# The opening of a fused two-block kernel in halves, with four of sixteen modulation tiles as two passes of rounded parts

## What is computed

```python
mod = silu(c) @ w_ada + b_ada            # c and c_ctx; shift = columns 0..1023, scale = columns 1024..2047
h   = rmsnorm(x, norm_mix) * (1 + scale) + shift        # for x with c, for ctx with c_ctx; 256 tokens each, D = 1024
p   = h @ w_in                                          # 39 column tiles of 128
```

## Time and profile before

| | |
|---|---|
| time, median of 3 (lowest, highest) | 1807.76 us (1807.01, 1810.53) |
| the profiled execution | 1811.46 us, span 1809.5 us |
| PE busy | 1758.9 us, 97% |
| DVE busy | 1306.0 us, 72% |
| ACT busy | 1050.5 us, 58% |
| mean granted clock of TensorE | 0.990 |

### The profile page before, as it was taken

One profiled execution on the slowest core, in us unless ns is written; L12 is line 12 of the kernel. 1 busy time (PEld: TensorE's weight loads), 2 busy tenths in 40 slices (PEclk: granted clock), 3 DMA queues, 4 the chain that ended last, 5 costly groups with the idle time before them and its releaser, 6 DMA issues.

```text
span 1809.5 us, 34945 instructions
## 1 busy us (share of the span) xinstructions
PE 1758.9 (97%) x11968; PEld 1588.0 (88%) x11968; DVE 1306.0 (72%) x2592; ACT 1050.5 (58%) x2110; POOL 180.1 (10%) x148
## 2 busy tenths in 40 slices
PE   7999999999899999999999999999999999999998
PEld 1878789999899988888899999999889899999997
DVE  3787457667898979766766666666686757878887
ACT  2545543343456679766655555555657666666666
POOL 0000003410673520000000000000010000010000
PEclk9899999999999999999999999999999999999999
DMA  8533223225445531255555555555444534455553
GB/s 296 182 105 106 82 83 105 82 98 174 150 164 176 179 110 36 94 195 190 196 185 186 187 188 186 188 189 186 162 174 141 191 126 140 166 182 186 185 185 128
DMA packets 77273, 283.34 MB, mean 157 GB/s; under 512 B 8576, under 2 KB 8576, under 8 KB 76928
## 3 DMA queue, kind: packets, MB, share of 16 engines
q1 hardware_dynamic: 77184, 282.16, 45.9%
HBM read 281.08 MB, written 1.05 MB: 156 GB/s over the span
## 4 chain that ended last, share of the span: by engine, by line
PE 82%; DVE 11%; ACT 3%; issue 1%; DMA 1%; POOL 1%; PEld 0%; PEldq 0%; ACTq 0%; SPq 0%; POOLq 0%; DVEq 0%
PE banks L867 19%; PE banks L855 16%; PE banks L946 9%; PE banks L455 8%; PE banks L1102 7%; PE banks L1126 3%; PE banks L646 2%; PE banks L627 2%; DVE split L2314 2%; PE banks L797 2%; DVE arena L2310 2%; PE banks L423 1%; PE banks L635 1%; PE banks L960 1%; DMA arena<-wstream 1%
## 5 line engine op out<-in xcount | busy, mean ns | idle before, releaser
L1444 ACT ACTIVATE split<-arena 128x512 fp32r<-128x512 f32 x492 | 309.0, 629 | 135.0 <-PE banks L855 76.8
L855 PEld LDWEIGHTS banks<-split 128*128 128x128 f32 x2880 | 355.4, 192 | 10.4 <-DVE split L2240 3.1
L867 PE MATMUL banks<-split 128*128 128x512 f32 x1536 | 361.9, 390 | 1.0 <-issue 1.0
L855 PE MATMUL banks<-split 128*128 128x256 f32 x2880 | 358.7, 283 | 3.1 <-DVE split L2240 2.3
L2332 DVE TENSOR_TENSOR split<-arena,split 128x512 fp32r<-128x512 f32 x396 | 270.7, 690 | 105.5 <-ACT split L1444 99.7
L867 PEld LDWEIGHTS banks<-split 128*128 128x128 f32 x1536 | 283.8, 188 | 57.3 <-issue 1.4
L1422 ACT ACTIVATE split<-arena 128x512 fp32r<-128x512 f32 x312 | 194.5, 628 | 117.1 <-PE banks L1102 52.9
L946 PE MATMUL banks<-split 128*128 128x256 f32 x1728 | 217.7, 287 | 4.3 <-DVE split L2410 3.9
L946 PEld LDWEIGHTS banks<-split 128*128 128x128 f32 x1728 | 212.3, 194 | 7.8 <-issue 6.0
L2387 DVE TENSOR_TENSOR split<-arena,split 128x512 fp32r<-128x512 f32 x180 | 123.2, 695 | 66.5 <-ACT split L1422 64.9
L455 PEld LDWEIGHTS banks<-split 128*128 128x128 f32 (+1 forms) x936 | 132.9, 193 | 28.1 <-issue 14.1
(11 more groups left out here) (413 smaller groups left out, 2447.9 us busy)
## 6 DMA issues: line engine op xcount, KB each, us to landing
arena<-wstream SPq DMA_DIRECT2D x525, 512.0 KB, 3.3
arena<-x_t SPq DMA_DIRECT2D x1, 2048.0 KB, 12.8
arena<-matsa SPq DMA_DIRECT2D x1, 1234.0 KB, 6.2
out_t<-arena SPq DMA_DIRECT2D x4, 256.0 KB, 2.0
arena<-mats SPq DMA_DIRECT2D x1, 576.0 KB, 7.9
arena<-crow SPq DMA_DIRECT2D x1, 512.0 KB, 7.0
arena<-rows SPq DMA_DIRECT2D x1, 512.0 KB, 4.0
arena<-mats SPq DMA_DIRECT2D x1, 449.0 KB, 4.3
```

Of the source, the lines that this page charges most:

```text
L855: mm = pe.matmul(ps[:, 4 + b, 0:S], w_parts[:, c, (2 * m + half) % 4, P * k:P * k + P], h_parts[:, e, 4 * half + k, :], start=(half == 0 a ...
L867: mm = pe.matmul(ps[:, 2 * tt + half, :], g_parts[:, e, j % 2, P * tt:P * tt + P], w_parts[:, c, (2 * m + half) % 4, :], start=(first and ...
L1444: act.activation(w_parts[:, 0, (2 * m + half) % 4, :], ring[:, peer_slot(m), 512 * half:512 * half + 512], ACT.Copy).then_inc(sem["w_hi"], 1)
```

## The change

The opening is put in another order, by halves of k:

- **Load order.** mats is no longer loaded ahead of tile 0, but after the modulation's tile 5. The host lays the four groups of w_ada in the order shift 0..511, scale 0..511, shift 512..1023, scale 512..1023, so that the first two groups give all that k 0 to 3 need.
- **Four columns.** silu(c) is stored with two columns of zeros beside it (csT, four columns), and as high and low part side by side (c_parts, four columns). Every modulation matmul now has four stationary columns and four output rows. For tiles 7, 9, 10 and 12 (MOD_SPLIT) the weights are split too: ScalarE writes the high part of the whole tile (mod_hi, 128 x 1024), VectorE the low part (mod_lo), and TensorE makes four fp32r matmuls (high and low of the weights, for each k) instead of two f32 ones. They use the same buffers w_parts as the projection.
- **Columns.** The rows of modrow are turned into columns by two accumulating f32 matmuls with parts of the identity for each 128 columns, which also add the two halves (mod_columns), instead of by one transpose; once after tile 5, 8 and 12, and the last inside in_tile(0) at k = 2.
- **Halves.** VectorE forms the gains twice, of k 0 to 3 and k 4 to 7 (gains). TensorE works column tiles 0 and 1 as k 0 to 3 of both, then k 4 to 7 of both.
- **Work moved to ScalarE.** Modulation of x for k 0 to 3, 6 and 7 and of ctx for k 4 to 7 (modulated, one ACT instruction each). ScalarE's squares now stand behind mod_out(0). VectorE's inversion and normalisation of ctx stand behind column tile 1's low parts.
- The last load of rows counts on another semaphore.

```diff
+MOD_SPLIT = (7, 9, 10, 12)
+MOD_HALVES = 2 * len(MOD_SPLIT)
+HALVES = MOD_HALVES + 2 * 39
...
+        c_parts = split[:, 4 * KT * S:4 * KT * S + 4 * KT].rearrange("p (k e) -> p k e", k=KT)
...
-            sp.dma_start(mats, mats_in).then_inc(sem["params_in"], 16)
...
-            load_freed_by_matmuls(RING, N_WIN + RING)
+            for n in range(RING, RING + 2):
+                sp.wait_ge(sem["tiles_done"], n - RING + 1)
+                sp.dma_start(tile_at(n), wstream[n]).then_inc(loaded[n % RING], 16)
+            sp.dma_start(mats, mats_in).then_inc(sem["mats_in"], 16)
+            load_freed_by_matmuls(RING + 2, N_WIN + RING)
...
-            pe.wait_ge(sem["silu_c"], 1)
-            for i in range(2):
-                for half in range(2):
-                    pe.wait_ge(sem["mod_bank_free"], 2 * i + half + 1)
-                    for q in range(4):
-                        pe.wait_ge(loaded[q], 32 * i + 16 * half + 16)
-                        for k in range(2):
-                            mm = pe.matmul(ps[0:2, half, :], csT[:, 2 * q + k, :], ring[:, q, 512 * k:512 * k + 512],
-                                           start=(q == 0 and k == 0), stop=(q == 3 and k == 1))
-                        mm.then_inc(sem["tiles_done"], 1)
-                    if i and half == 0:
-                        sum_squares(0, 512)
-                for half in range(2):
-                    pe.wait_ge(sem["mod_bank_free"], 2 * i + half + 3)
-                    for t in range(8 * i + 4 * half, 8 * i + 4 * half + 4):
-                        mm = pe.transpose(ps[:, 2, 2 * t:2 * t + 2], modrow[0:2, P * t:P * t + P], ident[0:2, 0:2])
-            mm.then_inc(sem["mod_cols"], 1)
-
-            def in_tile(t, among={}):
+            def mod_tile(n):
+
+                out = ps[0:4, n // 4 % 2, :]
+                if n in MOD_SPLIT:
+                    m = MOD_SPLIT.index(n)
+                    pe.wait_ge(sem["in_lo"], 2 * m + 2)
+                    for k in range(2):
+                        for c in range(2):
+                            mm = pe.matmul(out, c_parts[:, 2 * (n % 4) + k, :], w_parts[:, c, 2 * (m % 2) + k, :],
+                                           start=(n % 4 + k + c == 0), stop=(n % 4 == 3 and k + c == 2))
+                else:
+                    pe.wait_ge(loaded[n % RING], 16 * (n // RING + 1))
+                    for k in range(2):
+                        mm = pe.matmul(out, csT[:, 2 * (n % 4) + k, :], ring[:, n % RING, 512 * k:512 * k + 512],
+                                       start=(n % 4 + k == 0), stop=(n % 4 == 3 and k == 1))
+                mm.then_inc(sem["tiles_done"], 1)
+
+            def mod_columns(g):
+
+                pe.wait_ge(sem["mod_bank_free"], 2 + g + 1)
+                for j in range(4):
+                    out = ps[:, 2 if g < 2 else 6, 8 * (g % 2) + 2 * j:8 * (g % 2) + 2 * j + 2]
+                    row = modrow[0:4, 512 * g + P * j:512 * g + P * j + P]
+                    pe.matmul(out, row, ident[0:4, 0:2], start=True, stop=False)
+                    mm = pe.matmul(out, row, ident[0:4, 2:4], start=False, stop=True)
+                if g % 2:
+                    mm.then_inc(sem["mod_cols"], 1)
+
+            pe.wait_ge(sem["silu_c"], 2)
+            for n in range(16):
+                if n % 4 == 0:
+                    pe.wait_ge(sem["mod_bank_free"], n // 4 + 1)
+                mod_tile(n)
+                if n == 5:
+                    pe.wait_ge(sem["mats_in"], 16)
+                    mod_columns(0)
+                elif n == 6:
+                    sum_squares(0, 512)
+                elif n in (8, 12):
+                    mod_columns(n // 4 - 1)
...
-            for t in range(19):
+            in_tile(0, {2: (mod_columns, 3)}, range(4))
+            in_tile(1, {}, range(4))
+            in_tile(0, {}, range(4, KT))
+            in_tile(1, {}, range(4, KT))
+            for t in range(2, 19):
...
-            act.wait_ge(sem["params_in"], 32)
-            act.activation(csT, col("c2", KT, 2), ACT.Silu).then_inc(sem["silu_c"], 1)
-            act.wait_ge(sem["x_in"], 16)
-            for k in range(KT):
-                act.activation(sq[:, k, :].rearrange("p (c t) -> p c t", c=2), xc[:, :, k, :], ACT.Square).then_inc(sem["squares"], 1)
-
+            act.wait_ge(sem["params_in"], 16)
+            link(act.activation(csT[:, :, 0:2], col("c2", KT, 2), ACT.Silu))
+            act.activation(c_parts[:, :, 0:2], csT[:, :, 0:2], ACT.Copy).then_inc(sem["silu_c"], 1)
             def mod_out(i):
                 act.wait_ge(sem["tiles_done"], 4 * i + 4)
-                act.activation(modrow[0:2, 512 * i:512 * i + 512], ps[0:2, i % 2, :], ACT.Copy).then_inc(sem["mod_bank_free"], 1)
+                act.activation(modrow[0:4, 512 * i:512 * i + 512], ps[0:4, i % 2, :], ACT.Copy).then_inc(sem["mod_bank_free"], 1)
...
+            def mod_hi(m):
+
+                n = MOD_SPLIT[m]
+                act.wait_ge(loaded[n % RING], 16 * (n // RING + 1))
+                if m >= 2:
+                    act.wait_ge(sem["tiles_done"], MOD_SPLIT[m - 2] + 1)
+                act.activation(w_parts[:, 0, 2 * (m % 2):2 * (m % 2) + 2, :].rearrange("p s n -> p (s n)"), ring[:, n % RING, :], ACT.Copy).then_inc(
+                    sem["in_hi"], 2)
+
             mod_out(0)
+            act.wait_ge(sem["x_in"], 16)
+            for k in range(KT):
+                act.activation(sq[:, k, :].rearrange("p (c t) -> p c t", c=2), xc[:, :, k, :], ACT.Square).then_inc(sem["squares"], 1)
+            act.wait_ge(sem["mats_in"], 16)
+            act.activation(small[:, 84:85], eps, ACT.Sqrt)
+            mod_hi(0)
+            roots(0, 512)
+            mod_hi(1)
             mod_out(1)
-            act.activation(small[:, 84:85], eps, ACT.Sqrt)
+            mod_hi(2)
+            mod_hi(3)
             mod_out(2)
-            roots(0, 512)
+
+            def modulated(c, k):
+
+                return act.activation(hT[:, k, S * c:S * c + S], hT[:, k, S * c:S * c + S], ACT.Identity, bias=modT[:, k, c:c + 1],
+                                      scale=gain1[:, c, k:k + 1])
+
+            act.wait_ge(sem["scaled"], 4)
+            for k in range(4):
+                o = modulated(0, k)
+            link(o)
+            for k in (0, 2):
+                act.activation(hp[:, 0, k:k + 2, 0:S], hT[:, k:k + 2, 0:S], ACT.Copy).then_inc(sem["h_hi"], 2)
+            act.wait_ge(sem["tiles_done"], MOD_SPLIT[-2] + 1)
+            in_hi(0, 0)
+            in_hi(0, 1)
             mod_out(3)
-            for h in range(4):
-                in_hi(h // 2, h % 2)
+            act.wait_ge(sem["tiles_done"], MOD_SPLIT[-1] + 1)
+            in_hi(1, 0)
...
-            for k in range(KT):
+            hp_hi(0, 4)
+            modulated(0, 6)
+            link(modulated(0, 7))
+            for k in range(5, KT):
                 hp_hi(0, k)
+            in_hi(1, 1)
             in_out(0)
             for k in range(4):
                 hp_hi(1, k)
             in_out(1)
-            for k in range(4, 6):
-                hp_hi(1, k)
-            in_out(2)
-            for k in range(6, KT):
-                hp_hi(1, k)
+            for k0 in (4, 6):
+                act.wait_ge(sem["scaled"], KT + k0 + 2)
+                modulated(1, k0)
+                link(modulated(1, k0 + 1))
+                for k in range(k0, k0 + 2):
+                    hp_hi(1, k)
+                if k0 == 4:
+                    in_out(2)
             for t in range(3, 20):
                 in_out(t)
             act.wait_ge(sem["late_in"], 48)
@@ -1817,7 +1886,18 @@
...
+            dve.memset(csT[:, :, 2:4], 0.0)
             link(dve.memset(pad, 0.0))
+            dve.wait_ge(sem["silu_c"], 1)
+            dve.tensor_tensor(c_parts[:, :, 2:4], csT[:, :, 0:2], c_parts[:, :, 0:2].bitcast(F32), ALU.subtract).then_inc(sem["silu_c"], 1)
+
+            def mod_lo(m):
+
+                n = MOD_SPLIT[m]
+                dve.wait_ge(sem["in_hi"], 2 * m + 2)
+                dve.tensor_tensor(w_parts[:, 1, 2 * (m % 2):2 * (m % 2) + 2, :].rearrange("p s n -> p (s n)"), ring[:, n % RING, :],
+                                  w_parts[:, 0, 2 * (m % 2):2 * (m % 2) + 2, :].bitcast(F32).rearrange("p s n -> p (s n)"),
+                                  ALU.subtract).then_inc(sem["in_lo"], 2)
...
-            dve.wait_ge(sem["roots"], 1)

             def normalise(c, k):
                 return dve.tensor_tensor(hT[:, k, S * c:S * c + S], xc[:, c, k, :], rstd[:, S * c:S * c + S], ALU.mult)
-
-            for c in range(2):
-                link(dve.reciprocal(rstd[:, S * c:S * c + S], root[:, S * c:S * c + S]))
-                for k in range(KT if c == 0 else 4):
-                    o = normalise(c, k)
-            link(o)
-            dve.wait_ge(sem["mod_cols"], 1)
-            link(dve.tensor_tensor(modT[:, 0:16, :], bank(2, 16, 2), bc(col("b_ada")[:, 0:16], 2, 2), ALU.add))
```

(75 more changed lines are left out.)

21 lines of the change are left out of this document (10 added, 11 removed).

## The result

The change makes the kernel slower by 0.3%: 1813.40 us, median of 10 runs (1812.52 to 1816.67), against 1807.74 us (1806.66 to 1811.19, 10 runs) for the kernel before; ratio 1.0030, 95% interval 1.0022 to 1.0038. The profiled execution took 1812.81 us, span 1811.0. Run again, the ratio was 1.0038 (1.0024 to 1.0052).

What follows compares the result with a forecast made beforehand. VectorE's low part was taken to bound column tile 4 and so the end; +1.1 us for the reordered opening and +3.4 for half clock gave +4.5, from 1807.76 to 1812.3 us, range 1805.0 to 1817.5.

Steps and rivals of the forecast that it cites:

- What sets the end: From column tile 4's start at 62.50 us the rest follows; VectorE's low part, ready at 62.39, bounds that start.
- rival 4: Opening: TensorE, not VectorE, sets column tile 4, which then comes 5.2 us earlier; 1802.6 us, chance 0.12.
- Start: Kernel start: with mats later, tile 0 lands at 6.7 instead of 8.08 us, TensorE's fifth tile at 17.0 instead of 18.22.
- Columns: TensorE's thin column matmuls: 16 records a group, between 1.0 and 1.8 us, taken as 1.8; transposes before took 0.40.
- Rival 2: Columns cost only the transposes' 0.06 us a record: -1.6 us, in the middle 1809.0 us; chance 0.12.
- Split tiles: Modulation tiles 7, 9, 10, 12: 0.91 us each instead of 1.72 on TensorE, saving 3.2 us together.
- The stand ahead of tile 10: TensorE waits from 30.4 to 32.9 us, about 2.5 us, until VectorE's low part of modulation tile 10 releases it.
- The clock: TensorE falls to half clock around the stand ahead of tile 10, for 6.8 us, losing 3.4 us ahead of the gains.
- rival 3: Opening: clock falls more than once or for 10.2 us; +9.6 us, 1817.4; chance 0.16 together with late split parts.
- VectorE's stretch: From the second gains to column tile 4 VectorE takes 17.4 us instead of 19.6; column tile 4 at 63.6 without the clock.
- Sum: Column tile 4's delay: +1.1 us without the clock plus 3.4 for it, +4.5 us, column tile 4 at 67.0.
- VectorE's idle time of some 9 us: Ahead of the second gains VectorE stands some 9 us; inversion and normalisation of ctx would fit but are put behind.

Runs made afterwards that it cites:

- kernel before with its gap filled: Kernel before the change, plus four unused f32 matmuls of 512 columns between the last transposes and column tile 0; 1808.87 us, ratio 0.9994 to the kernel before.
- kernel with transposes: Changed kernel with no modulation tile split and columns made by one transpose per 128 instead of two f32 matmuls; 1807.56 us, ratio 0.9994 to the kernel before.
- the gap filled: Changed kernel plus two unused f32 matmuls of 512 columns ahead of modulation tile 10; 1812.67 us, ratio 1.0017 to the kernel before.
- ctx early: Changed kernel with inversion and all eight normalisations of ctx moved into VectorE's idle time ahead of the second gains; 1812.44 us, ratio 1.0016 to the kernel before.
- mats first: Changed kernel with the load of mats again ahead of modulation tile 0; 1816.65 us, ratio 1.0039 to the kernel before.

## Why the prediction was right

The forecast was slower, +4.5 us and 1812.3; measured are +5.7 and 1813.4. By its steps:

- **What sets the end.** Right: from 62.5 us on the rest of the kernel follows, 84.6 us to the first scores before and 84.9 after the change. The kernel before with its gap filled took 6.8 us of half clock away and nothing moved, so VectorE was the bound there, and with that rival 4 fell. In the changed kernel the trace puts the last 0.32 us ahead of column tile 4 to "issue" and not to VectorE; but VectorE's low part was ready at 66.1, 0.1 us before the start, while column tile 3 had ended at 65.88.
- **Start.** The mechanism was right, both sizes were off. Tile 0 came at 5.3, not 6.7: mats was worth 2.9 us there, not 1.4; why more than its bytes, stays open. But the fifth tile came at 16.34 (forecast 17.0), for it queues behind x and ctx; the new stand of 2.39 us was not in my walk.
- **Columns.** 16 records took 1.87 us (forecast 1.8, the dearer bound). Rival 2 is refuted in its price, and the kernel with transposes shows what the thin columns cost: 6.2 us over the four groups, the fall of the clock at their end included. By the row for 1 to 64 columns in the Trainium skill, "TensorE: Matmul & The Clock Gate", section "Back-to-back issue gap", it would have been 0.4 us a group. But that row is for matmuls alone; the same section says that in a stream of weight loads and matmuls both set the spacing. Every one of these records has its own load, so the prediction held the wrong row against the 1.87 us.
- **Split tiles.** 1.0 to 1.1 us each at full clock (forecast 0.91).
- **The stand ahead of tile 10.** 2.25 us from 30.3 to 32.55; forecast 2.5, from 30.4 to 32.9, released by VectorE's low part as forecast.
- **The clock.** It fell where I had it, at 32.5, but for 3.4 us, not 6.8: tiles 10 and 11 took 1.5 us more than with the gap filled, where I had 3.4. I had no second fall in the forecast; it came at 49.6, behind the last thin columns and a wait of 1.29 us, as rival 3 had it. In the changed kernel it cost VectorE 0.30 us of standing, with ctx early 2.07.
- **VectorE's stretch.** 18.3 us from 47.93 to column tile 4 at 66.20, not 17.4. Two terms were missing: the four modulations by ScalarE take 0.59 us each where I used the copy's 0.42 (rows below), 0.7 us together if all lie on the path, and the wait of 0.30 us for the high part behind column tile 0's copy.

```profile
L1233 ACT ACTIVATE arena<-arena 128x256 f32<-128x256 f32 x10 | 5.3, 587 | 1.4 <-DVE arena L1912 1.4
L1250 ACT ACTIVATE split<-arena 128x256 fp32r<-128x256 f32 x12 | 4.5, 411 | 6.2 <-DVE arena L1932 6.1
```

- **Sum.** In the profiled opening +3.7 us, where I had +4.5 (column tile 4 at 67.0, measured 66.20). The forecast was too late by 0.35 us up to tile 10 and by 1.9 for the fall. It was too early by some 0.5 for the split tiles and columns behind that, and by 0.9 for VectorE's stretch. So the mechanism and the sign were foreseen, but the closeness of the sum is in part luck: errors of 2.2 us one way and 1.4 the other. The medians differ by 5.7 (4.0 to 6.9 by the interval). Of the 2 us between the profiled opening and the medians no run shows the cause. The half-clock stretches that come and go are a likely one: without the fall at 245.8 the two profiled executions would lie 4.0 us apart, and the 1.7 us left are how far they stand from the medians of their kernels.

What I had not seen is how much lay in the order: I named VectorE's idle time of some 9 us (10.9 measured), but gave no price for using it.

## What to carry to other kernels

Before adding work that saves time on one engine, put its helpers' instructions in the queue by when the waiting engine wants them: here a low part of 1.2 us stood behind 2.8 us of normalisation that nobody was waiting for. TensorE's stand of 2.25 us and the clock's fall behind it (1.5 us) took back what four split tiles saved (some 3 us). Move what doesn't depend on the late result ahead of it: using VectorE's idle time before the second gains gave 2.5 us or more, where the split tiles gave nothing. And take the price of a thin matmul from rows with the same stationary load (0.11 us a record here), not from its columns, and watch what the granted clock does around it.

## What the runs showed of the hardware

- A f32 matmul of 2 moving columns with 4 rows and 128 stationary columns leaves two records and takes 2 x 0.112 us (16 records in 1.87 us). A transpose of two rows of the same block leaves one, and four take 0.34 us up to the next matmul.
- The stand of 2.25 us ahead of tile 10, behind thin columns and one split tile, is in four profiles (the changed kernel twice, ctx early, mats first). In each of them the granted clock fell from 1.0 to 0.50, at 32.5 to 33.1 us: at the stand's end in two, 0.5 us behind it in one, and 0.8 us after it began with mats first. With the same place filled by dense work it stayed at 1.0. A stand of 1.3 us ahead of column tile 0's second half is in eleven profiles: the clock fell there in the eight with thin columns before it, and in none of the three with transposes.
- The stand of 1.7 to 3.3 us for the fifth tile is in eleven profiles and lowered the clock in two of them only, so whether it falls there varies between executions or with the kernel; no run here tells which.
- 6.8 us at half clock less changed nothing where VectorE was the bound (54.2 us from the first matmul to column tile 4, and 54.3), and 3.4 us cost 1.5 where TensorE was.
- ScalarE's activation with a scale and a bias per partition takes 0.59 us on 128 x 256, its copy 0.41.
